# Gate turns in other stages' banks, two token tiles turned before the last down products, modulation tiles beside the value product

## What is computed

```python
mod_lat = (silu_c @ w_ada[i] + b_ada[i])[:, None, :]
sh_a, sc_a, g_a, sh_m, sc_m, g_m = jnp.split(mod_lat, 6, axis=-1)      # the same for the context
h_lat = x * (1.0 + sc_a) + sh_a
y_lat, y_ctx = gqa_mixer(...) if i % 2 == 0 else mla_mixer(...)        # mla: cq, ckv, k_pe = split(h @ w_in)
x = layer_norm(alpha * x + g_a * y_lat, ln_g[i, 0], ln_b[i, 0])
x = layer_norm(alpha * x + g_m * (square(relu((x * (1.0 + sc_m) + sh_m) @ w1)) @ w2), ln_g[i, 1], ln_b[i, 1])
```

## Time and profile before

| | us |
|---|---|
| median of three executions | 2246.8 |
| profiled execution, its own time | 2247.13 |
| its span | 2245.3 |
| TensorE busy (97% of the span) | 2176.8 |
| VectorE busy (56%) | 1253.7 |
| ScalarE busy (30%) | 670.2 |
| GpSimd busy (22%) | 485.2 |

### The profile page before, as it was taken

The page is one execution under the profiler, slowest core; times in us unless marked ns, Lnnn a source line. Parts: engine busy times, 40 slices in busy tenths (PEclk is TensorE's granted clock), DMA queues, the critical chain, the costliest instruction groups (busy, mean ns, idle before and its releaser), DMA issues.

```text
span 2245.3 us, 32724 instructions
## 1 busy us (share of the span) xinstructions
PE 2176.8 (97%) x13766; PEld 1770.9 (79%) x13766; DVE 1253.7 (56%) x1678; ACT 670.2 (30%) x1488; POOL 485.2 (22%) x259
## 2 busy tenths in 40 slices
PE   7999999999999999999999999999999999998998
PEld 7998878899889997788898645557888885556887
DVE  5676445855455864458654327665443443457566
ACT  2223443032012234440330368522102013362111
POOL 2222112334312221113343000101111110101332
PEclk9999999999999999999999999999999999999999
DMA  9533675646465437667465303022323233213551
GB/s 263 179 130 133 243 257 193 245 157 222 166 190 191 151 114 262 234 199 255 157 225 216 137 1 119 1 75 94 113 75 113 75 86 77 82 54 131 188 188 57
DMA packets 225958, 339.57 MB, mean 151 GB/s; under 512 B 58987, under 2 KB 94806, under 8 KB 225814
## 3 DMA queue, kind: packets, MB, share of 16 engines
q1 hardware_dynamic: 224720, 333.98, 43.0%
q0 software_dynamic: 944, 3.47, 0.4%
q10 hardware_dynamic: 150, 0.04, 0.0%
HBM read 335.38 MB, written 2.10 MB: 150 GB/s over the span
## 4 chain that ended last, share of the span: by engine, by line
PE 92%; DVE 4%; ACT 2%; SPq 1%; issue 1%; DMA 0%; POOL 0%; DVEq 0%; ACTq 0%
PE bank L282 22%; PE bank L284 22%; PE bank L283 21%; PE bank L2130 15%; PE bank L655 6%; PE bank L2133 2%; PE bank L1000 2%; PE bank L658 1%; SPq L222 1%; DVE ring_low L270 1%; PE bank L952 1%; DVE work L1704 0%; ACT work L1135 0%; DMA ring<-w_in 0%; DVE cos L2734 0%
## 5 line engine op out<-in xcount | busy, mean ns | idle before, releaser
L283 PE MATMUL bank<-hT_high,ring_low 128*128 128x256 f32 (+1 forms) x2048 | 606.0, 296 | 0.0
L283 PEld LDWEIGHTS bank<-hT_high,ring_low 128*128 128x128 f32 x2048 | 390.1, 190 | 12.1 <-issue 0.7
L263 POOL CAST ring_high<-ring 128x2048 fp32r<-128x2048 f32 (+1 forms) x108 | 204.7, 1895 | 675.9 <-PE bank L284 628.6
L270 DVE TENSOR_TENSOR ring_low<-ring,ring_high 128x2048 fp32r<-128x2048 f32 (+1 forms) x108 | 242.2, 2244 | 112.4 <-POOL ring_high L263 112.2
L282 PE MATMUL bank<-hT_low,ring_high 128*128 128x256 f32 (+1 forms) x1008 | 296.1, 294 | 6.9 <-DVE ring_low L270 5.2
L284 PE MATMUL bank<-hT_high,ring_high 128*128 128x256 f32 (+1 forms) x1008 | 285.6, 283 | 0.0
L263 POOL CAST half_high<-ring 128x2048 fp32r<-128x2048 f32 x64 | 128.4, 2010 | 635.7 <-PE bank L284 464.0
L282 PE MATMUL bank<-ring_low,hidden_high 128*128 128x512 f32 x640 | 251.2, 392 | 0.0
L1135 ACT ACTIVATE work<-bank 128x384 f32<-128x384 f32 (+11 forms) x246 | 109.8, 468 | 405.7 <-PE bank L284 359.7
L270 DVE TENSOR_TENSOR ring_low<-ring,half_high 128x2048 fp32r<-128x2048 f32 x64 | 152.7, 2391 | 97.0 <-POOL half_high L263 96.6
L282 PEld LDWEIGHTS bank<-hT_low,ring_high 128*128 128x128 f32 (+1 forms) x1008 | 192.8, 191 | 15.8 <-issue 8.5
(11 more groups left out here) (242 smaller groups left out, 4423.5 us busy)
## 6 DMA issues: line engine op xcount, KB each, us to landing
ring<-w_ff SPq DMA_DIRECT2D x32, 2048.0 KB, 8.1
ring<-mlp_w SPq DMA_DIRECT2D x32, 2048.0 KB, 7.9
ring<-w_in SPq DMA_DIRECT2D x30, 2048.0 KB, 8.7
ring<-w_ada SPq DMA_DIRECT2D x20, 2048.0 KB, 9.6
ring<-w_branch SPq DMA_DIRECT2D x24, 512.0 KB, 6.2
ring<-w_in SPq DMA_DIRECT2D x32, 256.0 KB, 4.2
ring<-w_out SPq DMA_DIRECT2D x4, 2048.0 KB, 8.7
work<-w_ada SPq DMA_DIRECT2D x4, 2048.0 KB, 13.6
```

The lines of the kernel that those rows point to most:

```text
L263: nc.gpsimd.tensor_copy(self.high(i), self.part(i, False)).then_inc(self.high_made, 1)
L270: nc.vector.tensor_tensor(self.part(i, True), self.part(i, False), self.high(i).bitcast(F32), ALU.subtract)\
L283: nc.tensor.matmul(out, a[1], b[0], start=False, stop=False)
```

## The change

Three things. The `ga` fills go to OT and the `gm` fills to SC; the first `gm` gate of each block is turned ahead of the up products instead of behind product 2, its `widen` ahead of VectorE's last modulation; the second keeps its place behind product 5. Tiles 0 and 1 of block 1 are turned ahead of token tile 3's last down products, and their modulation stands ahead of that tile's residual on VectorE; the last norm of block 0 now comes ahead of the next `widen`. In the hybrid layers' loop a modulation tile comes right ahead of `output(m-1)`, not behind its filler.

```diff
@@ filler and the loop of a hybrid layer (TensorE)
                 turn_gla(i - 2)
-            if i in ada_steps:
-                ada(ada_steps.index(i))
-
 
...
             if not later and m < PAIRS:
                 filler(2 * m + 1)
+            for i in (2 * m, 2 * m + 1):
+                if i in ada_steps:
+                    ada(ada_steps.index(i))
             if m >= 1:
                 output(m - 1)
 
@@ lists of fills
-            proj += [f"0xT2{h}" for h in range(2)] + ["0v1"] + gate_fills(0, "ga", 0) + ["0a0"] + gate_fills(0, "ga", 1)
-            proj += [f"0a{n}" for n in range(1, NORMED)] + ["0v0"]
+            proj += [f"0xT2{h}" for h in range(2)] + ["0v1"] + [f"0a{n}" for n in range(NORMED)] + ["0v0"]
...
-            proj += ["1cq0"] + gate_fills(1, "ga", 0) + ["1cq1", "1ckv0", "1ckv1", "1kpe"]
+            proj += ["1cq0", "1cq1", "1ckv0", "1ckv1", "1kpe"]
...
+        outs += [name for s in range(streams) for name in gate_fills(i, "ga", s)]
         outs += [f"{i}o{c}" for c in range(PAIRS)] + [f"{i}wo{t}{h}" for t in range(NT[i]) for h in range(2)]
+        score += [name for s in range(streams) for name in gate_fills(i, "gm", s)]
...
+    GATE = {"ga": OT, "gm": SC}
@@ turn_gate (TensorE); take_gate and widen likewise
-                ps = PROJ.claim(pe, name)
+                ps = GATE[kind].claim(pe, name)
...
-                last.then_inc(PROJ.full, 1)
+                last.then_inc(GATE[kind].full, 1)
@@ block loop (TensorE)
-            if i == 1:
-                turn_tiles(1, XT_ORDER[1][0:TT])
...
+            turn_gate(i, "gm", 0)
 
             per = UP_PER[i]
...
-                    for s in range(NT[i] // TT):
-                        if q == 0 and n == GM_AT[s]:
-                            turn_gate(i, "gm", s)
+                    if (i, q, n) == (0, 0, GM_AT):
+                        turn_gate(0, "gm", 1)
...
                     for b, t in order:
+                        if (i, q, h, b, t) == (0, QUARTERS - 1, 1, 0, NT[0] - 1):
+                            turn_tiles(1, XT_ORDER[1][0:TT])
@@ ScalarE
+            take_gate(i, "gm", 0)
             per = UP_PER[i]
...
-                    for s in range(NT[i] // TT):
-                        if q == 0 and n == GM_AT[s]:
-                            take_gate(i, "gm", s)
+                    if (i, q, n) == (0, 0, GM_AT):
+                        take_gate(0, "gm", 1)
@@ VectorE
             if i == 1:
+                layer_norm(0, 1, NT[0] - 1)
                 widen(1, "ga", 0)
-            for t in XT_ORDER[i][TT if i == 0 else 0:]:
-                if i == 1 and t == TT:
-                    layer_norm(0, 1, NT[0] - 1)
+            for t in XT_ORDER[i][TT:]:
                 modulate(i, f"{i}xT{t}1", t, 0, banks=row_banks(i, t))
...
+                if t == NT[i]:
+                    widen(i, "gm", 0)
                 if t >= 1:
                     banks = turn_banks(i, t - 1)
                     modulate(i, f"{i}hT{t - 1}1", t - 1, 3, hT_high, t == NT[i], banks)
...
-            widen(i, "gm", 0)
...
-                    if q == 0 and n == GM_AT[0] and NT[i] > TT:
-                        widen(i, "gm", 1)
+                    if (i, q, n) == (0, 0, GM_AT - 3):
+                        widen(0, "gm", 1)
...
                     for t in range(NT[i]):
+                        if (i, q, h, t) == (0, QUARTERS - 1, 1, NT[0] - 1):
+                            for xt in XT_ORDER[1][0:TT]:
+                                modulate(1, f"1xT{xt}1", xt, 0, banks=row_banks(1, xt))
                         residual(t, h, down_banks(h, t), f"{i}down{q}{h}{t}", ALPHA if q == 0 else 1.0)
```

More of the change, by code:

```diff
@@ L1946, in second_block @@
     UP_PER = [1, 2]
-    GM_AT = [2, 5]
+    GM_AT = 5
     QUARTERS = FFK // KD
@@ L1978, in second_block @@
                 proj.append(f"{i}up{q}_{n}")
-                for s in range(streams):
-                    if q == 0 and n == GM_AT[s]:
-                        proj += gate_fills(i, "gm", s)
             score += [f"{i}down{q}0{t}" for t in range(2)]
@@ L2445, in take_gate @@
             for h, name in enumerate(gate_fills(i, kind, s)):
-                ps = PROJ.arrived(act, name)
-                copy(gate_rows[:, s, 512 * h:512 * h + 512], ps[:, :]).then_inc(PROJ.free(name), 1)
+                ps = GATE[kind].arrived(act, name)
+                copy(gate_rows[:, s, 512 * h:512 * h + 512], ps[:, :]).then_inc(GATE[kind].free(name), 1)
         def scale_of(banks, name, part, o, mean):
@@ L2562, in scalar @@
             n_tok = buffers(i)[3]
-            for t in XT_ORDER[i][TT:] if i == 0 else XT_ORDER[i][0:TT]:
-                if i == 0 and t == 0:
-                    act.wait_ge(x_first, TT)
+            if i == 0:
+                act.wait_ge(x_first, TT)
+            for t in XT_ORDER[0][TT:] if i == 0 else XT_ORDER[1][0:TT]:
                 modulate(i, f"{i}xT{t}0", t, 0, banks=row_banks(i, t))
@@ L2601, in widen @@
                 i0, kind0, s0 = gate_order[gate_count[i, kind, s] - 2]
-                PROJ.taken(dve, *gate_fills(i0, kind0, s0))
+                GATE[kind0].taken(dve, *gate_fills(i0, kind0, s0))
             vec.tensor_copy(gate_src, src.to_broadcast([P, KD, P])).then_inc(gate_wide, 1)
@@ L2813, in vector @@
                 make(n)
-            PROJ.taken(dve, *gate_fills(i, "ga", NT[i] // TT - 1))
+            OT.taken(dve, *gate_fills(i, "ga", NT[i] // TT - 1))
             for t in range(NT[i] + 1):
@@ L2844, in vector @@
                 if q == 0:
-                    PROJ.taken(dve, *gate_fills(i, "gm", NT[i] // TT - 1))
+                    SC.taken(dve, *gate_fills(i, "gm", NT[i] // TT - 1))
                 dve.wait_ge(x_whole, whole_count[i, 0, NT[i] - 1])
```

## The result

| | before | after |
|---|---|---|
| median of its runs, us | 2247.26 (2245.05 to 2247.84, 4 runs) | 2231.02 (2228.35 to 2231.37, 4 runs) |
| profiled execution, us | 2247.13 | 2231.0 |
| its span, us | 2245.3 | 2229.2 |
| mean granted clock | 0.991 | 0.993 |

The ratio is 0.9927, 95% interval 0.991 to 0.9944: 16.2 us less, where 14.2 were forecast.

The account below looks back on a forecast made before the run. The prediction took TensorE, with 92% of the chain of waits, as the bound. It summed 8.1 (gates) + 7.2 (tiles 0 and 1) - 1.1 (modulation tiles) = 14.2 us off 2247.13, 2232.6 on the median's scale; range 2228 to 2240.

Parts of the forecast that it names:

- the clock: Half-speed stretches after the hT waits: up to 1.7 us each, 3.4 in all, if added turns count as activity; taken as 0.
- First MLP gates, 2 x 2.66: Each block's first MLP gate turns inside an existing wait before the up products, in empty banks: 5.3 us saved.
- Second MLP gate of block 0, 1.75: It keeps its place and its 0.9 us of turns, but its bank waits go: 1.75 us saved.
- Attention gates, 1.0: In free output banks, 0.74 us idle before the second fill goes, and 0.25 at the first gate: 1.0 saved.
- Part 2, 7.2: Block 1's tiles 0 and 1 at the join: 7.2 us saved, 3.5 wait, 0.7 bank wait, 2.65 slow clock, rest tails.
- the spare 0.7 on VectorE: At the join, VectorE's eight modulations end at 1865.6, the last down product at 1866.3: 0.7 us to spare.
- Part 3, +1.1: Six modulation tiles per layer move: 6, 14, 22 save 1.0 us, 8, 16, 24 cost 2.1 in sb waits; net 1.1 slower.
- Rival (a): Turns count for the clock, or idle phases fall luckily: 2229 us; chance 0.12.
- (b): At the join, modulation comes late or the clock drops for cq1: 1.7 to 2.9 us back, 2235; chance 0.08.
- (c): Score and output banks come free no sooner, gate waits return and `widen` is uncovered: 2238.6 us; chance 0.05.
- (d): In the layers' loop, modulation tiles wait for their loads, 3.4 x 6 = 20.7 us return: 2253, slower; chance 0.03.

Follow-up runs that it names:

- part 1 alone: Only the gate changes (other banks, first MLP gates turned earlier) put into the kernel before: 2236.35 us, ratio 0.9947.
- the kernel with VectorE late: Changed kernel, but VectorE modulates tiles 0 and 1 behind token tile 3's residual instead of ahead of it: 2237.52 us, ratio 0.9956.
- The kernel with part 3 alone: Only the move of modulation tiles ahead of `output` put into the kernel before: 2247.89 us, ratio 0.9999.
- 32 turns: Changed kernel with modulation tiles back behind their fillers, plus 32 thrown-away turns in block 1's wait before its first up product: 2230.16 us, ratio 0.9915.
- 8 matmuls: The kernel with 32 turns, with 8 float32 matmuls of 256 columns in their place in the same wait: 2228.68 us, ratio 0.9907.
- part 2 alone: Only the earlier turns and modulation of block 1's tiles 0 and 1 put into the kernel before, gates in the projection banks: 2243.66 us, ratio 0.9983.
- the miss with tiles 6, 14 and 22: Changed kernel with modulation tiles 8, 16 and 24 back behind their fillers, only 6, 14 and 22 moved: 2269.47 us, ratio 1.0097.

## Why the prediction was right, point by point

The forecast was 2232.6, the median is 2231.0; in the profiled pair 14.2 were summed and 16.1 found. Without the term that the prediction calls the clock, the terms measured come to 15.4 (5.32 + 1.90 + 1.69 + 7.34 - 0.9). Term by term:

- **First MLP gates, 2 x 2.66.** Right. In block 0 the way from the first up product to the one behind the gate went from 15.86 to 12.32. Of these 3.54, 2.66 are the gate and 0.88 the clock. The wait hid the turns, as said. The clock gave only 0.88 for 3.4 us at half speed because VectorE holds back the seventh matmul of the up products in both kernels, in after at 1508.02 with 0.70 of waiting, in before at the same time:
```profile
1508.01 0.58 PE L282 MATMUL bank<-hT_low,half_high 128*128 128x256 f32 x1 [0.22 <-DVE hT_low L2608]
```
What ran slowly ahead of it cost nothing. In block 1, 3.27 went; with 2.66 for the gate (2071.05 to 2073.71 in before) 0.61 is left for the clock. `widen` was hidden (VectorE still idles 1.53 behind it), but the turns ran at half clock: the first up product came 0.46 later behind the last tile's turns (2035.46 to 2039.57, so 4.11 against 3.65 before), and the seventh matmul waited 0.60 for VectorE. The length of the stretch isn't the reason for the 0.61: after has 3.4 us of it and part 1 alone 6.8, as before has, and both gain the same (3.27 and 3.28). What counts is how much of it lies behind the matmul that VectorE holds back.
- **Second MLP gate of block 0, 1.75.** 1.90.
- **Attention gates, 1.0: too small.** 1.69. Only the idle time ahead of the second fill had been counted, with 0.25 for the first gate. TensorE of before at both gates, with the products behind them:
```profile
1266.89 0.60 PE L2133 MATMUL bank<-consts,work 128*128 128x128 f32 x4
1267.74 0.66 PE L2133 MATMUL bank<-consts,work 128*128 128x128 f32 x4 [0.25 <-ACT work L2431]
1268.32 7.10 PE L2130 MATMUL bank<-work,ring 128*128 128x512 f32 x16
1275.26 0.60 PE L2133 MATMUL bank<-consts,work 128*128 128x128 f32 x4
...
1277.10 2.41 PE L2130 MATMUL bank<-work,ring 128*128 128x512 f32 x5
```
From first turn to the next product they went from 1.43 to 0.87 and from 1.84 to 0.87, 1.53 together; the other 0.16 of the stage stays unexplained. A gate split in two rows pays the second row's entry and tail as well as its wait.
- **Part 2, 7.2.** 7.34, with the spare 0.7 on VectorE measured at 0.7. That the cover carries it is shown by the kernel with VectorE late (6.3 back, forecast for a whole failure 2.6 or more). Part of the hit is luck, though. The term has 2.65 for slow clock, read from one execution with 6.8 us of it. The kernel with part 3 alone, whose instructions at the join are those of before, ran 3.4 us slowly there and took 8.67 for cq0 instead of 9.60:
```profile
1877.57 8.83 PE L2131 MATMUL bank<-work,ring 128*128 128x256 f32 x32 [3.54 <-DVE work L2622]
1886.24 0.60 PE L2134 MATMUL bank<-consts,work 128*128 128x128 f32 x4
```
Against that execution part 2 is worth 0.92 less.
- **Part 3, +1.1.** +0.9 is twice the 0.45 of the second layer, an assumption: in the first layer the same stage is 0.29 to 1.11 longer than in before even in kernels without part 3. In the second layer the wait was found alone (+1.01 for +1.05), the cheaper place of 6, 14 and 22 as a difference (-0.56 for -0.51).
- **The clock, taken as 0.** The one term whose reason failed. It gave about 1.5 at the two places (0.88 and 0.61) and took 0.7 over the rest of the program (16.1 - 15.4 - 1.5), where the change does nothing. The argument was that before 1868.4 turns alone didn't hold the clock. But behind those 16 turns TensorE was idle for 3.54, and the filled waits show, at block 1's entry, that it is the idle time that costs the clock: filled with turns or with matmuls, it runs at 1.00. Rival (a)'s mechanism is real; its size here was half of the 3.4 allowed. The Trainium skill ("TensorE: Matmul & The Clock Gate", Part 4) says that a transpose doesn't count as TensorE being busy the same way. For these float32 turns the runs disagree, and they decide here: 32 turns and 8 matmuls give the same clock and the same 220.44 us. The trace lists turns as MATMUL, so whether they ran in the mode that the page speaks of isn't shown.
- **Is it the extra 8 turns that hold the clock at 1507?** Likely, not always. All four kernels that turn the gate late (before, part 2 alone, part 3 alone, the gate behind up product 2) have a half-clock stretch within 1 us of the first up product; of the ten that turn it early, two (part 1 alone, and the one with matmuls in block 1) have one, 2 us behind it. That one is dearer, since it lies wholly behind the matmul that VectorE holds back: 13.84 from the first up product to the one behind the gate in both, not the 12.31 to 12.34 of the other eight.
- **The rivals.** (b) and (c) didn't happen, for the reasons given: 0.7 spare and no wait for line 2431 (2429 in after) at an up product. (d) didn't happen in after, where no row of line 1000 waits, but it was close. The load for tile 11 behind the moved tile 8, with SyncE's issue and the time to landing:
```profile
876.19 0.37 SPq L222 DMA_DIRECT2D ring<-w_ada  x1
...
ring<-w_ada SPq DMA_DIRECT2D x1, 2048.0 KB, 8.0
```
It landed at 884.2 and was used at 884.6, 0.4 later, although the gate's load issued at 864.64 took 13.5 and so overlapped it by some 2 us. The rival decides sooner than thought: the prediction asked which tiles come closer to each other in the change as a whole, and didn't see that its parts can't be taken one by one. That is what the miss with tiles 6, 14 and 22 cost.

Still open: why the clock falls at 1363 or 1366 in some executions of the same instructions and not in others. It can't be told from these traces, and it makes the 1 to 2 us between the best four kernels undecidable.

## What to carry to other kernels

A short fill whose bank is also the main loop's costs far more than its instructions (2.66 us for 0.9 of turns): give it a bank that has long been empty, and put it into a wait that is there anyway, after counting what the producing engines have spare. Before moving one of a row of tiles that share a load buffer, write down use-to-use times for every neighbour, moved and unmoved, and hold them against the load's landing time; a tile moved 4.7 us later left its successor 3.9 us for a load of 7.85. And where a stall on TensorE goes, look at the clock behind it, but book it apart from the mechanism.

## What the runs showed of the hardware

- Turns (float32, 128x128, through TensorE) keep the granted clock up as well as matmuls do: 0 of the 4 profiles with a filled wait at block 1's entry have half clock there, all 10 without do.
- Of two kernels with the same instructions up to 2028 us, one trace has a 10 us stretch at half clock (1.2 of 2.4 GHz) at 1366 and the other none; with the stretches elsewhere their mean granted clock is 0.991 and 0.997, and their spans differ by 8.8 us.
- At the join the same instructions took 44.52 us with 6.8 us at half clock (before) and 43.60 with 3.4 (part 3 alone).
- A slow stretch costs nothing where another engine sets the pace: VectorE held back the seventh matmul of block 0's up products to 1508.01 at a clock of 0.50 and to 1508.02 at 1.00.
- A load wait costs twice: 4.09 us of waiting, and the matmuls behind it at half clock (16 in 3.64 us instead of 1.93).
- A 2 MB load that went out 0.4 us ahead of another landed in 7.85 us, no slower than one alone; the one behind it took 13.5.
